# Routed experts: from rounds of two seats to items of 64 slots, with indirect row transfers

## The reference

```python
# 4 groups x 8 experts = 32 experts, TOP_E = 2, D_EXPERT = 512, 512 tokens
p_group = softmax(xf @ wr_g + br_g)
p_top, g_sel = top_k(p_group, 1)
fine = (xf @ wr_e + br_e)[the chosen group's 8 experts]
e_val, e_sel = top_k(fine, 2)
gate = p_top * softmax(e_val)              # one weight for each (token, expert) pair
expert_id = g_sel * 8 + e_sel
# each pair's row xb goes to its expert e:
y = (silu(xb @ w_gate[e]) * (xb @ w_up[e])) @ w_down[e]
out[token] += y * gate
```

## Time and profile before

| | us |
|---|---|
| median of 3 runs | 4006.45 |
| the runs | 4001.98 to 4007.94 |
| span of the profiled execution | 4008.1 |
| TensorE busy in it | 3480.4 (87%) |
| DVE busy | 1688.1 (42%) |
| ACT busy | 701.3 (17%) |
| POOL busy | 196.3 (5%) |
| bytes moved | 696.40 MB, 174 GB/s over the span |

### The profile page before, as it was taken

The page is one execution under the profiler, slowest core; times in us unless marked ns, Lnnn a source line. Parts: engine busy times, 40 slices in busy tenths (PEclk is TensorE's granted clock), DMA queues, the critical chain, the costliest instruction groups (busy, mean ns, idle before and its releaser), DMA issues. The chain is left out here.

```text
span 4008.1 us, 38008 instructions
## 1 busy us (share of the span) xinstructions
PE 3480.4 (87%) x13936; PEld 1752.2 (44%) x13937; DVE 1688.1 (42%) x3091; ACT 701.3 (17%) x1412; POOL 196.3 (5%) x263
## 2 busy tenths in 40 slices
PE   8998999888899999889889977778699978788775
PEld 4454434885444444378634432223243344422222
DVE  3235556775232555567548420000238766200002
ACT  1132204000112330310010100000122243100001
POOL 0001010001000001000000000000100130000000
PEclk9999999999999999899889989999889989799998
DMA  3115452004121226200143099999533421799996
GB/s 105 68 48 209 143 169 60 1 1 144 47 89 32 68 83 208 55 11 1 59 175 122 0 396 429 428 428 399 202 105 121 110 73 62 310 429 419 429 428 283
DMA packets 208086, 696.40 MB, mean 174 GB/s; under 512 B 22248, under 2 KB 105704, under 8 KB 182608
## 3 DMA queue, kind: packets, MB, share of 16 engines
q1 hardware_dynamic: 178576, 589.56, 38.4%
q0 software_dynamic: 29376, 105.05, 7.2%
HBM read 636.28 MB, written 58.28 MB: 173 GB/s over the span
## 5 line engine op out<-in xcount | busy, mean ns | idle before, releaser
L345 PE MATMUL bank<-fm,w 128*128 128x512 f32 (+1 forms) x912 | 397.3, 596 | 11.4 <-DMA w<-in_ab_w_in 6.3
L2796 PE MATMUL bank<-experts_wu,experts_hs 128*64 128x512 f32 x1120 | 275.8, 650 | 75.0 <-DMA experts_wu<-in_moe_w_up 75.0
L2796 PE MATMUL bank<-experts_wg,experts_hs 128*64 128x512 f32 x1120 | 272.2, 642 | 60.1 <-DMA experts_wg<-in_moe_w_gate 45.6
L345 PE MATMUL bank<-w,fm 128*128 128x512 f32 (+2 forms) x768 | 315.5, 567 | 6.5 <-DMA w<-in_w_in 6.5
L2861 DVE TENSOR_TENSOR fm<-bank,fm 128x512 f32<-128x512 f32 x35 | 37.0, 1056 | 638.9 <-PE bank L2796 638.9
L2796 PE MATMUL bank<-experts_wd,fm 128*64 128x512 f32 x1120 | 256.4, 611 | 45.4 <-issue 24.0
L345 PEld LDWEIGHTS bank<-fm,w 128*128 128x128 f32 (+1 forms) x912 | 172.4, 190 | 234.1 <-issue 221.0
L726 PE MATMUL bank<-fm,side_w 128*128 128x512 f32 x512 | 252.4, 619 | 6.9 <-DMA side_w<-in_w_in 5.4
L345 PEld LDWEIGHTS bank<-w,fm 128*128 128x128 f32 x768 | 142.2, 195 | 179.2 <-issue 153.8
L2796 PEld LDWEIGHTS bank<-experts_wu,experts_hs 128*64 128x64 f32 x1120 | 85.9, 148 | 263.2 <-issue 166.1
L2796 PEld LDWEIGHTS bank<-experts_wg,experts_hs 128*64 128x64 f32 x1120 | 94.6, 147 | 233.6 <-issue 230.5
(11 more groups left out here) (484 smaller groups left out, 4875.5 us busy)
## 6 DMA issues: line engine op xcount, KB each, us to landing
experts_wg<-in_moe_w_gate SPq DMA_DIRECT2D x64, 2048.0 KB, 19.5
experts_wu<-in_moe_w_up SPq DMA_DIRECT2D x64, 2048.0 KB
experts_wd<-in_moe_w_down SPq DMA_DIRECT2D x64, 2048.0 KB
ada_w<-in_ada_w POOLq DMA_DIRECT2D x96, 512.0 KB, 4.9
w<-in_w_in SPq DMA_DIRECT2D x40, 512.0 KB, 3.9
expert_rows<-fm POOLq DMA_DIRECT2D x35, 512.0 KB, 10.3
fm<-expert_rows SPq DMA_DIRECT2D x33, 512.0 KB, 21.6
w<-in_w_in SPq DMA_DIRECT2D x16, 1024.0 KB, 7.2
```

The lines of the kernel that those rows point to most:

```text
L345: ins = pe.matmul(bank, lhsT, rhs, start=(n == 0), stop=(n == len(todo) - 1))
L2796: ins = pe.matmul(bank[rows, :], lhs[:, k, rows], weights[:, s, k, cols], start=(k == 0), stop=(k == chunks - 1))
```

## The change

The stage "experts" is written anew.

- Work goes by items: 64 slots of one expert, all experts in their order 0 to 31 (`first` and `last` are running sums over all 32). Nothing is shared between two experts.
- Gate and up of one item stand side by side: both read the same 64 columns of `hs`; gate fills partitions 0 to 63 of bank 0, up partitions 64 to 127. The two halves of down do the same in bank 4.
- The down products of an item are made one item behind: TensorE's step p is: turn the hidden rows of item p-1, gate and up of p, turn the rows of p+1, down of p-1.
- `wg` and `wu` have two buffers each, used by even and odd experts; `wd` has one. SP's order is gate and up of e (after gate and up of e-2 are used), then down of e-1 (after the last down products of e-2).
- The normed tokens are stored to `token_rows` by SP in the stage before (`keep`). POOL gathers the 64 rows of an item as 128 half rows of 2 KB (half 0 on partitions 0 to 63, half 1 on 64 to 127) and scatters its y to `made_rows` in the same form. Both are indirect, with an index column copied from a table `at_from` or `at_to` by POOL; empty slots have an index out of bounds and are skipped. The table comes from a product of two 0/1 matrices.
- `made_rows` is in the order of the pairs, so that the closing stage reads it with eight plain loads of SP instead of eight gathers. The zero fill is gone.

The diff, cut to its core (`plan`'s arithmetic is left out):

```diff
@@ class Routed
+    def keep(self, sp, h):
+        for t in range(TILES):
+            sp.wait_ge(*self.norm.normed.at(t + 1))
+            sp.dma_start(self.chip.token_rows[t * P:(t + 1) * P, :], h[:, t, :]).then_inc(*self.chip.tokens_kept.inc(16))
@@ plan
+        pe.wait_ge(*marked.at(1))
+        product(pe, B[3][:, 0:ITEMS], [(at_slot[:, a, :], at_item[:, a, :]) for a in range(2 * TILES)]).then_inc(*tabled.inc())
@@ item_experts, sync
+        for e in range(EXPERTS):
+            if e == 2:
+                sp.wait_ge(*counted.at(1))
+            if e >= 2:
+                sp.wait_ge(*first_done.at(at(e - 2, END_AT, 1)))
+            load("moe_w_gate", e, wg[:, e % 2], gate_loaded[e % 2])
+            load("moe_w_up", e, wu[:, e % 2], up_loaded[e % 2])
+            if e == 0:
+                load_down(0)
+            if e >= 2:
+                sp.wait_ge(*down_done.at(at(e - 1, FIRST_AT, 1) + 1))
+                load_down(e - 1)
@@ item_experts, gpsimd
-            pool.wait_ge(*yready.at(p + 1))
-            pool.dma_start(rows[bass.ds(p * P, P), :], y[:, :]).then_inc(*ystored.inc(16))
-            pool.wait_ge(*ystored.at(16 * p + 16))
-            pool.sem_inc(yfree.sem, 1)
+        def fetch(p, picked, number):
+            pool.tensor_copy(now_from[:, :], at_from[:, bass.ds(p, 1)]).then_inc(*picked.inc())
+            pool.wait_ge(*placed.at(1))
+            pool.wait_ge(*picked.at(number))
+            pool.indirect_dma_start(out=xs[:, :], out_offset=None, in_=token_halves,
+                                    in_offset=bass.IndirectOffsetOnAxis(ap=now_from[:, 0:1], axis=0),
+                                    bounds_check=2 * SEQ - 1, oob_is_err=False).then_inc(*rows_loaded.inc(16))
+        def spread(q):
+            pool.wait_ge(*placed.at(1))
+            pool.wait_ge(*picked_to.at(q))
+            pool.wait_ge(*y_ready.at(q))
+            pool.indirect_dma_start(out=made_halves, out_offset=bass.IndirectOffsetOnAxis(ap=now_to[:, 0:1], axis=0), in_=y[:, :],
+                                    in_offset=None, bounds_check=4 * SEQ + 1, oob_is_err=False).then_inc(*y_stored.inc(16))
+            pool.wait_ge(*y_stored.at(16 * q - 16))
+        with pool.Fori(2, n + 2) as q:
+            pool.wait_ge(*rows_turned.at(q - 1))
+            fetch(q - 1, picked_from, q)
+            pick_to(q - 2)
+            spread(q)
+            pool.sem_inc(y_free.sem, 1)
@@ item_experts, tensor
+        turn(0)
+                with pe.Fori(first, end) as p:
+                    turn_hidden(p)
+                    pe.wait_ge(*gate_loaded[s].at(16 * j + 16))
+                    pe.wait_ge(*up_loaded[s].at(16 * j + 16))
+                    gate_and_up(p, s)
+                    turn(p + 1)
+                    pe.wait_ge(*down_loaded.at(landed))
+                    down(p)
@@ experts, moe_residual
-                    pool.indirect_dma_start(out=rows[:, at, :], out_offset=None, in_=made,
-                                            in_offset=bass.IndirectOffsetOnAxis(ap=row_of[:, at:at + 1], axis=0)
-                                            ).then_inc(*fetched[at].inc(16))
+                    sp.dma_start(rows[:, at, :], chip.made_rows[at * P:(at + 1) * P, :]).then_inc(*fetched[at].inc(16))
```

More of the change, by code:

```diff
@@ L2757, in _, with load, at @@
-        load_rows(2)
-        with sp.Fori(2, n) as p:
-            seats = first_two(p)
-            sp.wait_ge(*gathered.at(p))
-            load_rows(p + 1)
-            load("moe_w_down", wd, down_done, down_loaded, p, seats)
+        def load(name, e, into, landed):
+            sp.dma_start(into, io[name][i, e].rearrange("(p k) n -> p k n", p=P)).then_inc(*landed.inc(16))
+        def at(e, where, low):
+            return sp.value_load(counts[0:1, where + e:where + e + 1], min_val=low, max_val=ITEMS - 1)
@@ new lines, in down @@
+        def down(p):
+            pe.wait_ge(*hmoved.at(p + 1))
+            pe.wait_ge(*y_ready.at(p + 1))
+            for f in range(FC):
+                for d in range(2):
+                    ins = pe.matmul(B[4][d * SLOTS:(d + 1) * SLOTS, :], hidT[:, f, :], wd[:, f, d * BANK:(d + 1) * BANK],
+                                    start=(f == 0), stop=(f == FC - 1))
+            ins.then_inc(*down_done.inc())
+        turn(0)
+        pe.wait_ge(*counted.at(1))
+        with pe.Fori(0, EXPERTS // 2) as j:
+            for s in range(2):
+                first, end = (pe.value_load(counts[0:1, bass.ds(2 * j + (at + s), 1)], min_val=low, max_val=ITEMS - 1)
+                              for at, low in ((FIRST_AT, 0), (END_AT, 1)))
+                with pe.Fori(first, end) as p:
+                    landed = pe.value_load(counts[0:1, bass.ds(p + DOWN_AT, 1)], min_val=16, max_val=16 * EXPERTS)
+                    turn_hidden(p)
[5 more added lines that the diff above has]
+                    down(p)
@@ new lines, in experts, with _ @@
+                loaded.append(st.count("down_loaded", fresh=True))
+                @st.block.scalar
+                def _(act):
+                    for half in range(2):
+                        rows = slice(half * SLOTS, (half + 1) * SLOTS)
+                        act.activation(gate_half[rows, :], mod[rows, 5, half * BANK:(half + 1) * BANK], ACT.Copy).then_inc(*gated.inc())
+                route(chip, st, lg, choice, weight, routed, routed_ready)
+                plan(chip, st, fm, choice, routed, routed_ready, at_from, at_to, placed, counts, counted)
@@ L2912, in experts @@
+                item_experts(chip, st, i, io, fm, counts, counted, at_from, at_to, placed, gate_half, gated, hs, weights, loaded)
         used = chip.take_dirty()
```

365 lines of the change are left out of this document (144 added, 221 removed).

## The result

The changed kernel takes **4633.3 us** (median of 4 runs, 4620.8 to 4643.4), the kernel before on the same chip 4007.2 (4 runs, 4002.0 to 4016.6): ratio **1.157**, 95% interval 1.154 to 1.159. The profiled execution has a span of 4635.0 us, against 4008.1 before: +626.9. The forecast was 4535 with a range of 4180 to 4680, and slower with a chance of 0.88. Direction and range held, and so did the mechanism but for what ends the gather's landing and one wait at the end of each layer; the amount was 97 us too small.

What follows compares the result with a forecast made beforehand. Transfers at 428 GB/s bound the kernel before; afterwards a loop of scatter, gather, turn and down would. Layers +275 and +260, closings -5, sum +530 on 4006.5, rounded 4535 us; range 4180 to 4680.

Steps and rivals of the forecast that it cites:

- E: Moment: end of an item's down products. As rival: gate and up not side by side, 14.2 instead of 7.1 us.
- Scatter: POOL's store of y: issued 1.4 us after down products, landing 7.4 us (4 live pieces an engine) to 10.1 (8).
- GpSimd's turn: On POOL, from the scatter's landing to the next gather's issue: register work and index copy, 1.2 us in all.
- Gather: Next item's rows land 1.0 to 2.6 us after the weights' backlog ends at E+15.3: E+16.3 to 17.9.
- Turn, down and clock: TensorE turns the rows and makes down products, 4.4 us, plus 2.6 (0 to 4.2) for the clock lowered by idling.
- The sum: Full item period 16.9 + 4.4 + 2.6 = 23.9 us; 55 such periods, 11 of 20 us, plus starts and ends.
- Starts and ends: First gate product of the expert stage 4 us later; closing stage with plain loads 5 us shorter for both layers.
- Short periods: The 11 items with none to 2 MB of weights beside them: 14.3 us with nothing, 22 with a down load, taken 20.
- B: Rival: same loop but milder, rows pass the weights sooner and clock stays up; full period 19.5 us, 4260 us, chance 0.25.
- C: Rival: loop hides and weights bind if both landings stay under 8.3 us; period 15.3 us, 4000 us, chance 0.12.
- D: Rival: all slots moved and clock low throughout; period 26.5 us, 4680 us or more; D and beyond, chance 0.08.
- The two rules of the Trainium skill: Scatter landing: 2.0 us plus bytes, no traffic term (2.6 us); or 9 to 17 descriptors drained per ring turn (some 5).

Runs made afterwards that it cites:

- Short weights: Changed kernel, but only 256 KB instead of 2 MB loaded of every weight matrix after the first ones; 3980.8 us, ratio 0.988 to the kernel before.
- gather ahead: Changed kernel, but GpSimd gathers the next rows once the buffer is turned, ahead of everything for y; 4052.5 us, ratio 1.012 to the kernel before.
- gather first: Changed kernel, but GpSimd waits for the scatter's landing behind the next gather's issue, not ahead of it; 4267.4 us, ratio 1.060 to the kernel before.
- Two down buffers: The kernel gather ahead plus a second buffer for the down matrix; 4030.8 us, ratio 1.006 to the kernel before.
- gates first: Changed kernel, but SyncE issues the next expert's gate and up ahead of the late down matrix; 4613.0 us, ratio 1.145 to the kernel before.

## Why the prediction was right, and where its sizes were off

**The bound moved as said.** Weights and rows at 428 GB/s bound the kernel before; afterwards a loop of two landings does, with the DMA share at 0.62 to 0.64 (forecast near 0.65) and the transfers at work in the first 17 us behind E (forecast 15). Short weights and gather ahead show it from both sides. With shorter landings the waits for them shrink from 18.8 to 5.5 us an item; with the landings out of the loop, at the same bytes, nearly all of the loss is gone.

**Scatter.** Forecast issued at E+1.4, landed at E+8.8 to 11.5; measured E+1.6 and E+9.9. The value holds but its reasoning does not. I took 4 live pieces an engine against 8. Each transfer has 80 packets whatever is skipped, and live slots change the landing by 0.015 us each. The row of 10.3 us was the right neighbour, that the arithmetic from it came out right was luck.

**GpSimd's turn.** Forecast 1.2 us, measured 1.0 (copy 0.18, then 0.83 to the issue).

**Gather: the step that failed.** Forecast issued at E+10.0 to 12.7, there at E+16.3 to 17.9, because it ends 1.0 to 2.6 us behind the weights' backlog. It was issued at E+11.0 as said and there at E+18.5. In the changed kernel alone the rule could still stand, with a backlog that ends at E+17 instead of E+15.3 and rows 1.5 us behind it. But the backlog was the wrong clock: gather first put the issue at E+3.7 and had the rows at E+13.1, some 4 us before the weights' last packets. The term is 7.5 us from issue, not 5.6 (the middle of the forecast range is 17.1, not the 16.9 that the sum used). What makes it 7.5 here and 9.5 there was not found. The trace's landings of the gathers and then of the scatters, 2350 to 2850 us:

```profile
DMA to landing us min/median/max: 3.3/7.5/7.9
...
DMA to landing us min/median/max: 7.3/8.1/9.0
```

**Turn, down and clock.** Forecast 4.4 + 2.6 = 7.0 us, measured 5.8 in the item shown and 6.4 by the group means (turn 1.08, down 372.0 / 70 = 5.3). The mechanism stands, its price is 2.1.

**The sum.** A full period has 25.5 us instead of 23.9: +1.9 from the gather, -0.6 from turn and clock, and the rest in small steps. Between the scatters there are 57 distances of this length (28 of 35 in layer 0, 29 of 33 in layer 1; the forecast had 27 and 28). With the nine short ones (forecast 11 of 20 us) and without the last of each layer they sum to 1614 us, where the forecast had 55 x 23.9 + 11 x 20 = 1534: +79.

The forecast left out one wait. The last item has no gate and up of its own, but its down matrix may be loaded only behind the down products before it, and takes longer than all that stands ahead of its use. The last down products of layer 1:

```profile
4590.19 5.50 PE L2803 MATMUL bank<-experts_wd,fm 128*64 128x512 f32 x16 [8.00 <-DMA experts_wd<-in_moe_w_down]
```

From the E before them to the last scatter 17.0 and 16.0 us pass in the two layers, where the forecast had 6.4: +20. Two down buffers takes this wait away and gains 19 us by it. The first E comes 8 us earlier than forecast in layer 0, and 4 us in layer 1, the closing of layer 0 counted in: -12. Behind the last scatter the kernel takes 4.0 us more than before, where the forecast had 5 less for both closings: +9. That is 96 of the missing 97 us. The last scatters stand at

```profile
3183.40 1.00 POOL L2753 DMA_INDIRECT made_rows<-fm,now_to  x1 [0.85 <-POOL now_to L2747]
...
3192.42 4.44 SPq L2913 DMA_DIRECT2D rows<-made_rows  x8
...
3196.38 2.67 DVE L2930 SCALAR_TENSOR_TENSOR x<-rows,experts_weight,x 128x1024 f32<-128x1024 f32 x2 [14.18 <-DMA rows<-made_rows]
```

and at 4597.62, where the earlier trace rows has 2871.68 and 3974.66: +311.7 and +311.2 us for the two layers, forecast +275 and +260.

**Starts and ends.** Forecast +4 for the first start and -5 for the two closings. The first gate product stands at 2334.7, 2.8 us earlier than in the earlier trace rows; the first add of the closing stage comes 13.0 us after the last scatter, was 10.8. The plain loads are quick, but SyncE issues them only 9.0 us behind the scatter's issue, where GpSimd's gathers stood 6.4 us behind the store. From the last scatter to the end of the span 37.4 us pass, 33.4 before. Small, of the wrong sign both times.

**Short periods.** With no weights 13.0 to 13.6 us (forecast 14.3), with one matrix 18.6 to 21.0 (forecast 22, taken 20).

**The rivals.** B (19.5 us a period) is excluded by 25.5 in the changed kernel; gather first happens to have its time, from one landing less in the loop. C would have needed both landings under 8.3 us together; they took 8.4 and 7.6. With short weights they are under it, and the time falls below that of before. D (26.5) is 1.0 us above what was measured; the clock was low for the down products, but up for gate and up. E did not happen: gate and up end by E+8, in the same 7 us as the two-seat rounds.

The two rules of the Trainium skill, page DMA: Bandwidth & Descriptors, gave estimates of 2.6 us for the scatter among weights (section Anatomy of one DMA) and some 5 us (section Queues, rings and completion order). The first is near the landings without traffic: 2.7 us for the last scatter of layer 0, 3.3 us for the one in the period of 13.0. Among weights both are too short, with a median of 8.1 us. It is this landing that is against the second; the equal counts of the earlier trace rows are sums over 16 engines, and could look alike if each engine drained its pieces in one go at a time of its own.

## What to carry to other kernels

A transfer may be small and cheap and still cost its whole landing if what it brings is needed in the same iteration in which it is issued; multiply the landing *under the traffic that the loop itself starts* by the iterations. Here two transfers of some 0.13 MB cost 9 to 10 us an item, and moving the issue of one of them one iteration ahead gave back nine tenths of it, without a byte less. Order the queue of an engine so that what the next iteration needs never stands behind a wait for what this one has finished; and count the clock that idle time takes from the instructions behind it.

## What the runs showed of the chip that was not expected

- An indirect transfer of 64 slots in half rows has 80 packets on the software queue, skipped slots or not: 26032 over the kernel with 68.93 MB and with 88.80 MB. Its landing depends little on them (7.2 us of waiting with 2 live slots, 8.4 with 61).
- A small indirect gather beside weight loads lands 7.5 us after issue in the changed kernel, 8.4 in gates first and 9.5 in gather first (medians), there some 4 us before the last packets of the weights. With the weights cut to an eighth GpSimd's wait for the scatter is 3.3 us, with none it is 2.3.
- Queue counts, 2577 to 2582 us, the landing of one scatter: all 80 packets pass within 5 us, the first of them some 4 us after the issue at 2573.4, while the weights keep 95% of the engines' time. What the queue does in these 4 us no run here shows.

```profile
q1 hardware_dynamic: 140, 2.03, 94.9%
q0 software_dynamic: 80, 0.09, 4.8%
```

- TensorE with 12 unread products an item is busy 97% of the stretch, and the kernel is 60 (by the times) to 90 us (by the ratios) faster for it: the granted clock stays at 1.00 (2.4 GHz) where it fell to 0.50 (1.2 GHz) in the idle stretch.
